# One block for the last three stages: second half of the key pass, combination of the experts, last norm

## The reference, cut to what matters

```
act = gelu(einsum('td,thkd->thk', hb, u_tab[eidx]))
out = einsum('thk,thkd->td', gates * act, v_tab[eidx])
x = x + gt2 * out
return rmsnorm(x, final_norm_w)
```

## Time and profile before

| | us |
|---|---|
| median of 3 runs | 2917.51 (2910.99 to 2920.88) |
| the profiled execution | 2909.72 |
| its span | 2908.0 |
| PE, DVE, ACT, POOL busy in the span | 2670.9, 1963.0, 1041.0, 1287.0 |
| last matmul of the key pass ends | 2317.04 |
| first matmul of the combination starts | 2344.93 |
| last matmul of the combination ends | 2883.80 |

### The profile page before, as it was taken

How to read it: one execution, slowest core, us unless ns; L and a number is a source line. 1 busy time by engine, 2 the same in 40 slices (tenths; PEclk the granted TensorE clock), 3 DMA queues, 4 the chain that set the end, 5 groups by cost and what they waited for, 6 DMA issues and landing times. The chain is left out here.

```text
span 2908.0 us, 38560 instructions
## 1 busy us (share of the span) xinstructions
PE 2670.9 (92%) x14085; PEld 2248.1 (77%) x14085; DVE 1963.0 (68%) x3122; ACT 1041.0 (36%) x1653; POOL 1287.0 (44%) x607
## 2 busy tenths in 40 slices
PE   7998999799999989888798999999999879999996
PEld 5887877555778878667586799999999758887885
DVE  4445232687754453465655287769999789999998
ACT  4322321355233223321122133335555433443442
POOL 3443442111334434333143367772222157777773
PEclk9999999899999999999799999999999989999998
DMA  5443342112234433222002255549999999999993
GB/s 175 138 151 119 109 155 66 41 62 91 90 116 151 144 131 107 72 102 73 1 23 72 89 166 169 164 133 378 348 346 336 326 334 373 376 373 379 373 378 135
DMA packets 189995, 535.16 MB, mean 184 GB/s; under 512 B 14272, under 2 KB 96576, under 8 KB 169792
## 3 DMA queue, kind: packets, MB, share of 16 engines
q1 hardware_dynamic: 83520, 298.95, 31.4%
q0 software_dynamic: 18432, 134.23, 11.8%
q10 hardware_dynamic: 87936, 100.68, 10.0%
HBM read 478.22 MB, written 55.57 MB: 184 GB/s over the span
## 5 line engine op out<-in xcount | busy, mean ns | idle before, releaser
L345 POOL TENSOR_TENSOR ring_low<-ring,ring_high 128x1024 fp32r<-128x1024 f32 x323 | 796.5, 2469 | 1105.6 <-ACT ring_high L312 1105.6
L396 PE MATMUL ps<-u_high,ring_high 128*128 128x512 f32 (+1 forms) x1728 | 658.9, 381 | 43.3 <-DVE u_low L636 17.4
L397 PE MATMUL ps<-u_low,ring_high 128*128 128x512 f32 (+1 forms) x1728 | 650.5, 376 | 0.0
L398 PE MATMUL ps<-u_high,ring_low 128*128 128x512 f32 (+1 forms) x1728 | 649.8, 376 | 0.0
L312 ACT ACTIVATE ring_high<-ring 128x1024 fp32r<-128x1024 f32 x355 | 374.6, 1055 | 616.0 <-PE ps L398 546.2
L396 PEld LDWEIGHTS ps<-u_high,ring_high 128*128 128x128 f32 x1728 | 328.0, 190 | 105.5 <-issue 40.9
L398 PEld LDWEIGHTS ps<-u_high,ring_low 128*128 128x128 f32 x1728 | 328.1, 190 | 49.2
L397 PEld LDWEIGHTS ps<-u_low,ring_high 128*128 128x128 f32 x1728 | 328.4, 190 | 48.7 <-issue 2.0
L2420 POOL DMA_INDIRECT fetched_rows<-in_peer_uv,fetch_index x128 | 165.0, 1289 | 339.5 <-DVE ps L2440 302.5
L345 POOL TENSOR_TENSOR ring_low_more<-ring,ring_high_more 128x1024 fp32r<-128x1024 f32 x96 | 245.3, 2567 | 32.1 <-ACT ring_high_more L312 31.5
L2975 DVE TENSOR_TENSOR expert_coef_low<-expert_product,expert_coef_high 128x384 fp32r<-128x384 f32 x128 | 214.7, 1677 | 0.1
(11 more groups left out here) (436 smaller groups left out, 4939.0 us busy)
## 6 DMA issues: line engine op xcount, KB each, us to landing
ring<-in_peer_u SPq DMA_DIRECT2D x128, 512.0 KB, 4.1
ring<-in_peer_uv SPq DMA_DIRECT2D x128, 512.0 KB, 6.6
ring<-in_ffn_gu SPq DMA_DIRECT2D x88, 512.0 KB, 3.6
ada_weights<-in_ada_w SPq DMA_DIRECT2D x48, 512.0 KB, 3.9
ring<-in_ffn_down SPq DMA_DIRECT2D x48, 512.0 KB, 3.6
expert_acts<-kept_acts ACTq DMA_DIRECT2D x128, 192.0 KB, 4.2
expert_weights<-weight_stage ACTq DMA_DIRECT2D x24, 1024.0 KB, 8.9
group_acts<-expert_acts ACTq DMA_DIRECT2D x16, 1536.0 KB, 17.6
```

Source lines behind the costliest of these rows:

```text
L345: pool.tensor_tensor(k.lows[p], k.ring[:, s], k.highs[p].bitcast(F32), ALU.subtract)\
L396: pe.matmul(out, k.highs[p][:, w], high, start=first, stop=False)
L397: pe.matmul(out, k.highs[p][:, w], low, start=False, stop=False)
L398: last = pe.matmul(out, k.lows[p][:, w], high, start=False, stop=final)
```

## The change

- `weigh`, `combine` and the last norm are put into one block. Between them no engine waits for the others, other than by the semaphores named in the code. `weight_stage` now lives as long as the block, and the routing's two tables of candidates are laid into it.
- ACT doesn't wait for the last stores of `weigh` before it loads. The activations and gates of group 0 come in two steps, two experts (EDGE) first and then six. Gates are read from DRAM for 23 of the 24 blocks (NB - 1): the last one is copied for groups 0 and 1 by ACT from `weight_stage`, so its store needn't have landed. With two experts a piece has 128 bytes, with six 384 bytes, and each step has 23 x 128 = 2,944 of them.
- DVE waits for the first step and the copied block at chunk 0, and for the second step at chunk 2. Group 1 is loaded after ACT's first table splits.
- The first 128 tokens are finished as soon as DVE has added their last row, the other three blocks as soon as PE has finished each (`tokens_done` after the 6 last matmuls of each). The squares are summed by ACT (Square), with a Sqrt and a reciprocal for each block, and the scaling of block b comes after the sum of block b+1. Each is stored when it is ready. A Sqrt on a constant stands ahead of it.

```diff
-                load(0)
-                load(1)
-                for j in range(1, WIDE):
-                    stream.split_high(act, 0, j)
-                for n in range(WIDE):
-                    coef_high(n)
...
+            load_acts(0, 0, EDGE, first_acts)
+            act.wait_ge(x.staged[0].sem, 16 * (NB // 2))
+            load_weights(0, NB - 1, 0, EDGE, first_weights)
+            load_acts(0, EDGE, 8, acts_loaded[0])
+            load_weights(0, NB - 1, EDGE, 8, weights_loaded[0])
+            for g in range(2):
+                copy = act.activation(weights[:, g, NB - 1].rearrange("p (e t) -> p e t", t=WT), x.stage[:, 1, 8 * g:8 * g + 8],
+                                      ACT.Copy)
+            copy.then_inc(last_block.sem, 1)
+            for j in range(1, WIDE):
+                stream.split_high(act, 0, j)
+            for s in range(ACTS):
+                act.wait_ge(x.stored[s].sem, 16 * (P // ACTS))
+            load_acts(1, 0, 8, acts_loaded[1])
+            load_weights(1, NB - 1, 0, 8, weights_loaded[1])
+            for n in range(WIDE):
+                coef_high(n)
...
+            act.wait_ge(eps_ready.sem, 1)
+            act.activation(root[:, 0:1], eps[:], ACT.Sqrt)
+            for b in range(QT):
+                act.wait_ge(rows_summed.sem, b + 1)
+                act.activation(junk, rows[:, b], ACT.Square, accum_out=squares[:, b:b + 1]).then_inc(squared.sem, 1)
+                act.wait_ge(squared.sem, b + 1)
+                act.activation(root[:, b:b + 1], squares[:, b:b + 1], ACT.Sqrt, scale=1.0 / D, bias=eps[:]).then_inc(rooted.sem, 1)
...
+            def scale(b):
+                dve.wait_ge(rooted.sem, b + 1)
+                step(dve.reciprocal(root[:, b:b + 1], root[:, b:b + 1]))
+                dve.scalar_tensor_tensor(rows[:, b], rows[:, b], root[:, b:b + 1], final, ALU.mult, ALU.mult)\
+                   .then_inc(rows_ready.sem, 1)
+
+            dve.memset(eps[:], EPS).then_inc(eps_ready.sem, 1)
+            dve.wait_ge(x.added.sem, CHOICES)
+            for b in range(QT):
+                bank = 6 if b < GB else 2 * (b - GB)
+                if b >= GB:
+                    dve.wait_ge(tokens_done.sem, b - GB + 1)
+                for half in range(2):
+                    ins = dve.tensor_tensor(gated[:, b % 2, half * T:(half + 1) * T], k.ps[:, bank + half],
+                                            gates[half][:], ALU.mult)
+                step(ins)
+                dve.tensor_tensor(rows[:, b], rows[:, b], gated[:, b % 2], ALU.add).then_inc(rows_summed.sem, 1)
+                if b == 0:
+                    dve.wait_ge(final_loaded.sem, 16)
+                if b >= 1:
+                    scale(b - 1)
+            scale(QT - 1)
...
-            weigh(k, x, choices, acts)
-        combine(k, x)
+            with k.nc.Block() as block:
+                weigh(k, x, choices, acts, block)
+                mid.close()
+                combine(k, x, block)
```

More of the change, by code:

```diff
@@ L2390 @@
 HALVES = DT // HT // U_ITERS
+EDGE = 2
 class Experts:
@@ new lines, in _, with take @@
+        @block.sync
+        def _(sp):
+            stream.load(sp)
+        @block.tensor
+        def _(pe):
+            stream.multiply(pe)
+        @block.gpsimd
+        def _(pool):
+            for c in range(fetched + FETCHED - 2):
+                x.fetch(k, pool, c)
+        @block.scalar
+        def _(act):
+            for b in range(2):
+                act.sem_inc(taken[b].sem, 1)
+            def take(i, e):
+                for q in halves_at(e + 1) if e < 7 else []:
+                    h = i * HALVES + q
+                    b, slot, part = h % 2, h // 2 % 2, h % 2
+                    act.wait_ge(weighed[b].sem, h // 2 + 1)
+                    if part == 0 and h >= 4:
+                        act.wait_ge(x.staged[slot].sem, 16 * (h // 4))
+                    act.activation(stage[:, slot, :, part * HT:(part + 1) * HT].rearrange("p e t -> p t e"),
+                                   k.ps[:, 2 * b:2 * b + 2].rearrange("p b (t e) -> p (b t) e", e=P), ACT.Copy)\
+                       .then_inc(taken[b].sem, 1)
+                    if part == 1:
+                        act.wait_ge(taken[b].sem, taken[b].at(h // 2 + 1))
+                        act.dma_start(k.dram["expert_weights"][h // 2],
+                                      stage[:, slot].rearrange("p e t -> p (e t)")).then_inc(x.staged[slot].sem, 16)
+                if GB and 1 <= e < 7:
+                    x.gate_row(act, i * PER_U + e - 1)
+            keep_acts(k, x, act, stream, acts, EARLY, (4, 5), take)
@@ L2868, in weigh, with combine @@
         stream.finish()
-def combine(k, x):
+def combine(k, x, block):
     nc = k.nc
@@ new lines, in multiply, with _ @@
+                if final:
+                    last.then_inc(tokens_done.sem, 1)
+            if not final:
+                last.then_inc(k.used[p].sem, 1)
+        @block.sync
+        def _(sp):
+            stream.load(sp)
+            sp.dma_start(final, k.dram["final_rows"]).then_inc(final_loaded.sem, 16)
+            for b in range(QT):
+                sp.wait_ge(rows_ready.sem, b + 1)
+                sp.dma_start(k.dram["y"][b], rows[:, b]).then_inc(stored.sem, 16)
+            sp.wait_ge(stored.sem, 16 * QT)
@@ new lines, in _, with fetch_up_to @@
+        @block.gpsimd
+        def _(pool):
+            issued = fetched + FETCHED - 2
+            def fetch_up_to(n):
+                at = issued
+                while at < CHOICES and v_place(at - FETCHED + 2) + 1 <= n:
+                    x.fetch(k, pool, at)
+                    at += 1
+                return at
+            for i in range(V_ITERS):
+                for j in range(1, 9):
+                    if 8 * i + j < P:
+                        stream.low_chunk(pool, i + j // 8, j % 8)
+                    issued = fetch_up_to(8 * i + j)
@@ new lines, in _, with split @@
+        @block.vector
+        def _(dve):
+            step = lambda ins: k.dve_steps.then(dve, ins)
+            def split(n):
+                dve.wait_ge(high_ready.sem, n + 1)
+                dve.tensor_tensor(low[:, n % WIDE], product[:, n % 3], high[:, n % WIDE].bitcast(F32), ALU.subtract)\
+                   .then_inc(low_ready.sem, 1)
+            for n in range(P):
+                b, e = n // 8 % 2, n % 8
+                if n == 0:
+                    dve.wait_ge(first_acts.sem, 16)
+                    dve.wait_ge(first_weights.sem, 16)
+                    dve.wait_ge(last_block.sem, 1)
+                if n == EDGE or (e == 0 and n > 0):
+                    dve.wait_ge(acts_loaded[b].sem, 16 * (n // 16 + 1))
+                    dve.wait_ge(weights_loaded[b].sem, 16 * (n // 16 + 1))
+                if n >= 3:
+                    dve.wait_ge(low_ready.sem, n - 2)
+                dve.tensor_tensor(product[:, n % 3].rearrange("p (b t) -> p b t", t=WT),
+                                  acts[:, b, e].rearrange("p (b t) -> p b t", t=WT),
+                                  weights[:, b, :, e * WT:(e + 1) * WT], ALU.mult).then_inc(product_ready.sem, 1)
+                if n >= 1:
+                    split(n - 1)
+                for c in range(fetched, CHOICES):
+                    if v_place(c) == n:
+                        x.take_row(dve, c)
+            split(P - 1)
+            for c in range(CHOICES - 2, CHOICES):
+                x.add_row(dve, c)
+            def scale(b):
[5 more added lines that the diff above has]
+            dve.wait_ge(x.added.sem, CHOICES)
+            for b in range(QT):
+                bank = 6 if b < GB else 2 * (b - GB)
[11 more added lines that the diff above has]
+            scale(QT - 1)
```

282 lines of the change are left out of this document (89 added, 193 removed).

## The result

| | median, us | executions | against before |
|---|---|---|---|
| before | 2916.68 (2907.97 to 2920.88) | 5 | |
| after | 2887.81 (2880.04 to 2895.30) | 5 | 0.9908 [0.9879, 0.9938] |

The profiled execution of after took 2895.3 us (span 2893.6), 14.4 less than that of before. A second profiled execution of the same program took 2886.3. Both are needed to see what happened.

What follows compares the result with a forecast made beforehand. PE's matmuls fill the combination, so only the two gaps, 52.1 us together, could yield: 5.7 + 10.1 = 15.8 us less, 2917.5 - 15.8 = 2902 us for the median, range 2893 to 2911.

Steps and rivals of the forecast that it cites:

- the combination still 539 us: Middle stretch, PE's first to last matmul of the combination: taken as untouched by the change, 538.87 us before.
- because DVE and POOL fall in with each other otherwise: Sign of a wrong forecast, in the combination: it would be longer by more than 3 us.
- The first gap: From the key pass to PE's first matmul of the combination: 5.7 us won, 1.3 to 11.1 by the bounds.
- The small pieces: Group 0's gates on ACT's queue: 3.2 us for pieces of 128 bytes, 3.9 us for those of 384 bytes.
- the 4.0 us for sharing: First gap: ring loads and most of a 1 MB fetch share the DMA engines, 4.0 us, 1.4 to 5.6.
- The rule of the 1,170: ACT's queue, first gap: an issue returns once no more than some 1,170 pieces of the transfers before it are left.
- The last gap: After PE's last matmul: 10.1 us won, 7.6 if Square and Sqrt needed different tables.
- The rivals: Queue doesn't hold ACT (2897.5, 0.10); start worth nothing (2907.4, 0.20); small pieces at twice 512-byte price (2914.5, 0.07); slower (0.03).
- once nor twice the 512-byte price: First gap: small pieces at 27.7 ns and more (second rival, 0.20) or at 55.4 ns (third rival, 0.07).
- A price of two pieces for one: Third rival, first gap: small pieces at 55.4 ns, PE 7.1 us later, 2914.5 us in all; chance 0.07.

Runs made afterwards that it cites:

- without that load: The changed kernel without the load of group 2, which is computed with group 0's activations and gates: 2880.89 us, 0.9892 of before.
- with the pause: The kernel before with one more wait: ahead of chunk 24 PE waits until DVE has split chunk 26; 0.9992 of before.
- the run that should have kept the lead in every execution: The changed kernel with one more wait: at chunk 17 PE waits until DVE has split chunk 18; 2886.87 us, 0.9917 of before.
- the tail alone: The kernel before with only the end changed, the last norm done token block by token block in the combination's block: 2905.63 us, 0.9971.
- before again: The kernel before, unchanged, under another name: 2911.43 us, 0.9992 of before.
- the two steps: The changed kernel with group 2's load also in two steps, experts 16 and 17, then 18 to 23: 2899.50 us, 0.9950 of before.
- coef_high(0) alone moved: The changed kernel with coef_high(0) alone put ahead of group 1's load on ACT: 2885.50 us, 0.9899 of before.

## Why the prediction was wrong

- **The step that failed: "In the second [stretch] it issues 2,304 matmuls in 538.87 us ...; the change doesn't touch this stretch", and "the combination still 539 us".** Its instructions are untouched, but not when they meet. By chunk 6 DVE is 7 us ahead of PE instead of 1, and one of after's two traced executions then ran at the short period: its combination took 528.8 us instead of 538.9. That the lead left behind group 2's landing decides is supported by the runs without that load and with the pause, and not proven: the run that should have kept the lead in every execution still had two of six above 2895 us. At the short period 8.1 + 10.1 + 10.5 = 28.7 us are won between the end of the key pass and the end, beside the measured 28.9. At the long one it is 7.25 - 1.93 + 10.49 = 15.8. That this is the sum forecast is luck: its terms were 5.7, 0 and 10.1. That after's median stands for the short period is inferred from its times; two of its executions were traced, one of each.
- The prediction did name the place among what would make it wrong ("because DVE and POOL fall in with each other otherwise"), but as a loss of more than 3 us, with no row read for it. The row was there, in the waits of before from 2345 to 2870 us:

```profile
PE ps L2902 <- DVE expert_coef_low L2975: 37.0, 16, 27.9
```

  Of these 37.0 us the longest, 27.9, is the gap, and 9 lie in 15 other stops. They come from the order in which the engines meet and not from work, and a change in who is first can remove them.
- **The first gap: right in sum, two sizes off against each other.** Group 1's last issue returned at 2334.98, 16.5 us behind the key pass; 20.9 had been forecast (2337.9). The small pieces were cheaper (13.3 ns taken as 17, 19.4 taken as 22.5), and of the 4.0 us for sharing little was seen: from 2322.5 to 2334.98 the rings' reloads moved nothing and POOL's fetch 3 packets. But from there to PE it took 4.1 us and not 1.3, since split(0) took 3.35 under POOL's remainders where 0.54 was set down. The sum gave 22.2 us and the gap was 20.6.
- **The rule of the 1,170 held for one issue and not for another.** 6,882 packets, and the 71 ahead of 2322.5, had gone of 7,936 when group 1's last issue returned: 983 left, near it. But the third issue was held until 2327.30, when 3,393 packets had gone since 2319.96, more than the 3,200 of the two experts. By the rule it would have come back with 2,000 gone. Why is open.
- **The last gap: right**, 10.5 us in the traces beside 10.1, with one table load and ACT behind DVE but for the fourth block. The times of the tail alone give 8.4.
- The rivals: none came out. Small pieces cost neither once nor twice the 512-byte price. The Trainium skill ("DMA: Bandwidth & Descriptors", Specifications) has pieces of 512 bytes as the least for full rate and says that smaller ones are read, modified and written. A price of two pieces for one does not show here: 128 bytes took 13.3 ns with the engines 73% busy for this queue alone, half of 27.7. A lower rate does at 128 bytes (9.6 bytes in a ns for one engine, 18.5 at 512), and not at 384 (19.8).

What stays open: what sets the border between the two periods. The lead at the last chunk of the group behind the last stop near the start goes with the period: 4.7 us or less was followed by the long one (before at 4.0, before again and after at 4.4, tail alone and the two steps at 4.7), 5.5 or more by the short one (5.5, 5.7, 5.8, 6.6 and 7.8). But it is no rule for every group. With coef_high(0) alone moved, the lead was 3.7 at chunk 39, and all groups stayed at 32.64. How many of after's untraced executions ran at which period is not known either.

## What to carry to other kernels

When a loop's engines wait for each other in turn, "the same instructions" is not "the same time": read who waits for whom over a whole period, and treat small stops that repeat (here some 0.9 us a group, in 13 to 16 groups) as a state that another start may leave. A change that only lets an off-path engine run ahead can pay more than the gap it shortens, and a late transfer can take it back. And a transfer issued from an engine that computes has a second price, the time for which its issue holds that engine: splitting one load into two cost more than waiting for it.

## What the runs showed of the hardware

- An issue on ACT's queue mostly took 0.4 to 2.3 us. It held ACT for 4.5 to 12.2 us as the third or fifth of a series, and for 5.3 to 9.3 us when the group before had not landed.
- An elementwise instruction of DVE of 0.55 us took up to 5.64 us under two of POOL's that stood back to back, in 15 of 47 cases of before; in the other 32 DVE got in between. It counts as busy for all of it. So DVE's busy time fell from 525.8 to 481.9 us with the same 500 instructions.
- A stop of 7.9 us on the busiest engine made the kernel no slower: 0.9992 [0.9982, 1.0003] of before.
